# Half of NSA's output projection moved into the last attention turn, an unscaled first convolution product, merged exponentials and another order of pieces

## The reference, cut to what matters

```python
def conv_mixer(a, state, w_in, w_conv, w_out):        # a = rmsnorm(x, g)
    gb, gc, v = jnp.split(a @ w_in, 3, axis=-1)
    u = gc * v
    ...
def nsa_merge(gates, o_c, o_s, o_w, w_out):
    o = gates[:, :, 0, ..., None] * o_c + gates[:, :, 1, ..., None] * o_s + gates[:, :, 2, ..., None] * o_w
    b, t = o.shape[:2]
    return o.reshape(b, t, N_HEADS * HEAD_DIM) @ w_out
```

## Time and profile before

| | us |
|---|---|
| median of 3 runs | 1237.3 (1236.7 to 1241.01) |
| the profiled execution, its own time | 1240.33 |
| its span, first to last instruction | 1238.6 |
| PE busy | 1179.3 (95%) |
| DVE busy | 476.5 (38%) |
| ACT busy | 282.7 (23%) |
| POOL busy | 220.8 (18%) |

### The profile page before, as it was taken

The page is one execution under the profiler, slowest core; times in us unless marked ns, Lnnn a source line. Parts: engine busy times, 40 slices in busy tenths (PEclk is TensorE's granted clock), DMA queues, the critical chain, the costliest instruction groups (busy, mean ns, idle before and its releaser), DMA issues.

```text
span 1238.6 us, 36557 instructions
## 1 busy us (share of the span) xinstructions
PE 1179.3 (95%) x14710; PEld 967.6 (78%) x14710; DVE 476.5 (38%) x1370; ACT 282.7 (23%) x755; POOL 220.8 (18%) x376
## 2 busy tenths in 40 slices
PE   8999999999999999999788779999999999999998
PEld 6877876999999977874345447797887987978966
DVE  2110115676775323005778773441121211211223
ACT  1000003110110022325877861310011011010131
POOL 4033242011340000413355540100000000000000
PEclk9999999999999999999999999999999999999999
DMA  9998889999442474653687789599999999999721
GB/s 328 307 311 282 300 284 320 170 364 334 141 163 97 179 288 154 175 104 102 205 278 241 240 259 356 216 375 366 378 343 368 362 366 393 334 353 389 295 102 39
DMA packets 122955, 329.99 MB, mean 266 GB/s; under 512 B 17864, under 2 KB 56729, under 8 KB 121124
## 3 DMA queue, kind: packets, MB, share of 16 engines
q1 hardware_dynamic: 96628, 259.88, 57.6%
q0 software_dynamic: 16656, 59.30, 16.5%
q10 hardware_dynamic: 9504, 8.48, 2.4%
HBM read 319.16 MB, written 15.70 MB: 270 GB/s over the span
## 4 chain that ended last, share of the span: by engine, by line
PE 80%; issue 6%; SPq 4%; DMA 4%; POOLq 2%; POOL 2%; DVE 1%; ACT 1%; DVEq 0%; ACTq 0%
PE bank L2715 16%; PE bank L2048 16%; PE bank L2155 12%; PE pbank L2726 6%; PE bank L2191 6%; PE pbank L2715 3%; PE bank L2726 3%; PE bank L2106 3%; PE bank L2259 3%; SPq L630 2%; POOLq L630 2%; DMA gring<-in_dense_gu 1%; PE bank L2667 1%; DMA gring<-in_conv_in 1%; SPq L640 1%
## 5 line engine op out<-in xcount | busy, mean ns | idle before, releaser
L2715 PE MATMUL bank<-X,gring 128*64 128x96 f32 x4608 | 197.5, 246 | 6.2 <-issue 5.8
L2715 PEld LDWEIGHTS bank<-X,gring 128*64 128x64 f32 x4608 | 192.6, 137 | 11.6 <-issue 11.4
L2048 PE MATMUL bank<-aT,gring 128*128 128x288 f32 x736 | 183.3, 407 | 4.9 <-DMA gring<-in_conv_in 3.1
L2048 PEld LDWEIGHTS bank<-aT,gring 128*128 128x128 f32 x736 | 138.9, 190 | 44.3 <-DMA gring<-in_conv_in 3.6
L2726 PE MATMUL pbank<-Q,X 128*32 128x256 f32 x1152 | 78.1, 379 | 0.0
L640 POOL DMA_DIRECT2D Q<-in_cache_cmp x96 | 51.8, 539 | 123.0 <-issue 123.0
L2155 PE MATMUL bank<-aT,gring 128*128 128x144 f32 x528 | 72.3, 286 | 0.0
L1974 DVE TENSOR_TENSOR X<-X,bank 128x96 f32<-128x96 f32 x72 | 18.4, 256 | 134.1 <-ACT X L1328 132.2
L1967 DVE TENSOR_TENSOR hT<-hT,bank 128x288 f32<-128x288 f32 x48 | 18.9, 449 | 129.0 <-PE bank L2667 129.0
L2155 PEld LDWEIGHTS bank<-aT,gring 128*128 128x128 f32 x528 | 67.8, 190 | 0.3 <-issue 0.3
L2048 PE MATMUL bank<-Q,gring 128*128 128x288 f32 x256 | 63.3, 408 | 1.3 <-ACT tS L957 0.7
(11 more groups left out here) (394 smaller groups left out, 1794.6 us busy)
## 6 DMA issues: line engine op xcount, KB each, us to landing
gring<-in_moe SPq DMA_DIRECT2D x176, 512.0 KB, 6.0
Q<-in_moe SPq DMA_DIRECT2D x72, 512.0 KB, 7.4
gring<-in_dense_gu SPq DMA_DIRECT2D x44, 512.0 KB, 12.4
gring<-in_conv_in SPq DMA_DIRECT2D x24, 512.0 KB, 7.2
Q<-in_cache_cmp POOLq DMA_DIRECT2D x96, 128.0 KB, 4.2
Q<-in_cache_cmp SPq DMA_DIRECT2D x96, 128.0 KB, 4.0
gring<-in_dense_down SPq DMA_DIRECT2D x16, 704.0 KB, 5.4
Q<-in_cache_cmp ACTq DMA_DIRECT2D x64, 128.0 KB, 3.8
```

What stands on the lines that cost most here:

```text
L2048: ins = pe.matmul(bank(label, k)[:, 0:T], tile[:, 128 * i:128 * i + 128], rhs[:, i, :], start=i == 0, stop=i == C - 1)
L2715: ins = pe.matmul(m_bank(i, M_GU + f)[64 * w:64 * w + 64, CAP * u:CAP * u + CAP], gslot(("m", 0), 2 * f + u)[:, o:o + 64], ae[:, c, :], st ...
```

## The change

Four edits.

1. **First product.** DVE makes xg0 = x times gain, without the factor 1/rms, while the squares are still summed; PE multiplies ("gc", 0) with xg0 right behind the norm, and DVE applies the factor when it takes the result out of the bank (ACT copied it before). The zeros are three, then one behind the second and one behind the fourth step of the norm. SP waits for ("gc", 0) before it loads w_cmp, which shares memory with xg0.
2. **Half of the output projection.** Head groups 0 to 3 are complete before turn 3. In turn 3, half_out(c) multiplies their 4 chunks of weights with the 256 prompt tokens for each of the 8 output chunks, and half_added(c) adds the bank to h. The final pass has 4 chunks by 288 tokens and 4 by the 32 sample tokens. The weights for it are loaded twice: four tiles ("wa", i) are put in the ring behind sv(2, 2) and behind sv(2, 3), each of two DMAs of 256 KB on SP.
3. **Merged exponentials.** The compressed branch of the prompt has one exponential of 32 columns instead of four of 8 with an accumulated sum; DVE subtracts the maxima first and sums afterwards.
4. **Order.** In each turn ACT does prompt_exps(2p, 0) ahead of key_scale(p, 2), and all five exponentials of the selected branch one after the other; PE does T6, window_keys, importance, T2, prompt_transposes, T5, prompt_transposes, T3, T4; DVE does window_scores behind prompt_transposed(2p, 0).

```diff
--- before.py
+++ after.py
@@ g_tile_order
             if p:
                 o += [("sv", p - 1, u, b2) for u in VALUES_AT[t] for b2 in range(2)]
+            if p == 3 and t >= 2:
+                o += [("wa", 2 * (t - 2) + i) for i in range(2)]
@@ g_released
+            elif kind == "wa":
+                full(eng, ("wa", 2 * label[1] + 1))
@@ sync
+            full(sp, ("gc", 0))
             for k in range(2):
                 sp.dma_start(wc[:, 32 * k:32 * k + 32, :], A["w_cmp"][:, 32 * k:32 * k + 32, :]).then_inc(wcmp_in, 16)
...
+                elif label[0] == "wa":
+                    n = GN[label]
+                    g_released(sp, g_labels[n - GS])
+                    for i in range(2):
+                        sp.dma_start(gslot(label)[:, 512 * i:512 * i + 512], A["nsa_out"][2 * label[1] + i][:, 0:512]).then_inc(g_in[n % GS], 16)
@@ scalar, prompt_exps
                 if i == 0:
-                    for w in range(2):
-                        for q in range(2):
-                            act.activation(Scp[:, w, q, :], Scp[:, w, q, :], ACT.Exp, bias=nmp[:, w, q, 0:1],
-                                           accum_out=smp[:, w, q, 0:1]).then_inc(pexp_ready, 1)
+                    act.activation(Scp, Scp, ACT.Exp).then_inc(pexp_ready, 1)
@@ scalar, turn p
                 key_scale(p, 1)
+                key_squares(p, 4)
+                key_squares(p, 5)
                 if p:
                     prompt_exps(2 * p - 1, 1)
                 if p == 0:
                     token_values(1)
-                key_squares(p, 4)
-                key_squares(p, 5)
-                key_squares(p, 6)
+                prompt_exps(2 * p, 0)
                 key_scale(p, 2)
...
                 exps(1, SN[p % 2], smt[:, 4:5], sexp_ready)
+                if p < 3:
+                    key_squares(p + 1, 1)
                 exps(1, S[:, 0:512], smt[:, 0:1], sexp_ready)
+                exps(1, S[:, 512:1024], smt[:, 1:2], sexp_ready)
+                exps(1, S[:, 1536:2048], smt[:, 3:4], sexp_ready)
+                exps(1, S[:, 1024:1536], smt[:, 2:3], sexp_ready)
@@ vector
             dve.wait_ge(first_in, 16 * NFIRST)
+            for c in range(C):
+                dve.wait_ge(x_in[c // 2], 16)
+                dve.tensor_scalar(xg0[:, c, :], hT[:, c, :], gains[:, c:c + 1], None, ALU.mult).then_inc(xg_sums_ready, 1)
             norm(0)
...
+            full(dve, ("gc", 0))
+            drain(dve.tensor_tensor(sg[:, 0, :], bank(("gc", 0))[:, 0:T], rs[:, 0, :], ALU.mult), ("gc", 0))
...
-                dve.wait_ge(pexp_ready, 12 * (k + 1))
+                dve.wait_ge(pexp_ready, 9 * (k + 1))
+                chain(dve.tensor_reduce(smp[:, :, :, 0], Scp, AX.X, ALU.add))
+                settled()
...
+            def half_added(c):
+                full(dve, ("wa", c))
+                drain(dve.tensor_tensor(hT[:, c, 0:TP], hT[:, c, 0:TP], bank(("wa", c))[:, 0:TP], ALU.add), ("wa", c))
@@ tensor
-            norm(0)
+            for c in range(C):
+                norm_step(0, c)
+                if c in (1, 3):
+                    warm(1)
+            g_arrived(pe, ("gc", 0))
+            for c in range(C):
+                pe.wait_ge(xg_sums_ready, c + 1)
+                ins = pe.matmul(bank(("gc", 0))[:, 0:T], gslot(("gc", 0))[:, 128 * c:128 * c + 128], xg0[:, c, :],
+                                start=c == 0, stop=c == C - 1)
+            fill(ins, ("gc", 0))
...
+            def half_out(c):
+
+                g_arrived(pe, ("wa", c // 2))
+                bank_free(pe, ("wa", c))
+                for k in range(4):
+                    drained(pe, ("po", k))
+                    o = 512 * (c % 2) + 128 * k
+                    ins = pe.matmul(bank(("wa", c))[:, 0:TP], gslot(("wa", c // 2))[:, o:o + 128], oT[:, k, 0:TP],
+                                    start=k == 0, stop=k == 3)
+                fill(ins, ("wa", c))
...
             for c in range(C):
-                g_linear(("wo", c), oT)
+                g_arrived(pe, ("wo", c))
+                bank_free(pe, ("wo", c))
+                for k in (4, 5, 6, 7, 0, 1, 2, 3):
+                    first = 0 if k >= 4 else TP
+                    ins = pe.matmul(bank(("wo", c))[:, first:T], gslot(("wo", c))[:, 128 * k:128 * k + 128], oT[:, k, first:T],
+                                    start=k == 4, stop=k == 3)
+                fill(ins, ("wo", c))
```

More of the change, by code:

```diff
@@ L562, in trunk @@
             other = by_pool(label) or label[0] in ("skip", "d")
-            landed.append((landed[n - GS] if n >= GS else 0) + (0 if other else 64 if four else 16))
+            landed.append((landed[n - GS] if n >= GS else 0) + (0 if other else 64 if four else 32 if label[0] == "wa" else 16))
             pool_landed.append((pool_landed[n - GS] if n >= GS else 0) + (64 if by_pool(label) else 0))
@@ L1005, in _ @@
             for c in range(C):
[L1006 removed]
                 if c >= 2:
                     drained(act, ("v", c - 2))
[L1009 removed]
+                if c:
+                    full(act, ("gc", c))
+                    drain(act.activation(sg[:, c % 2, :], bank(("gc", c))[:, 0:T], ACT.Copy), ("gc", c))
                 if c == 0:
+                    full(act, ("gc", 0))
                     pages(early_pages, 1)
@@ L1248, in _ @@
                     token_values(2)
+                key_squares(p, 6)
+                if p == 0:
                     folded_values()
                 transposed(p, 0)
-                prompt_exps(2 * p, 0)
                 key_squares(p, 7)
@@ L1278, in _ @@
                 transposed(p, 3)
-                if p < 3:
-                    importance(p + 1)
                 transposed(p, 4)
-                transposed(p, 2)
                 if p < 3:
@@ L2110, in _, with warm @@
             pe.wait_ge(constants_set, 1)
-            for _ in range(6):
-                pe.matmul(bank(("norm", 0))[:, 0:T], zeros[:, 0:128], zeros[:, 128:128 + T], start=True, stop=True)
+            def warm(n):
+                for _ in range(n):
+                    pe.matmul(bank(("v", 0))[:, 0:T], zeros[:, 0:128], zeros[:, 128:128 + T], start=True, stop=True)
+            warm(3)
             pe.wait_ge(first_in, 16 * NFIRST)
-            norm(0)
+            for c in range(C):
[8 more added lines that the diff above has]
+            fill(ins, ("gc", 0))
             for c in range(C):
                 for name in ("gc", "v", "gb"):
-                    g_linear((name, c), aT, ready=0 if c == 0 and name == "gc" else None)
+                    if (name, c) != ("gc", 0):
+                        g_linear((name, c), aT, ready=0 if (name, c) == ("v", 0) else None)
                 if c >= 2:
@@ L2583, in _ @@
                     selected_values(p - 1, 3)
+                if p == 3:
+                    half_out(0)
                 prompt_logits(2 * p + 1, 1)
+                if p == 3:
+                    half_out(1)
+                transposes(p, 6)
+                if p == 3:
+                    half_out(2)
                 if p < 3:
                     window_keys(p + 1)
-                transposes(p, 6)
-                transposes(p, 3)
-                if p < 3:
                     importance(p + 1)
                 transposes(p, 2)
+                if p == 3:
+                    half_out(3)
                 prompt_transposes(2 * p, 0)
+                if p == 3:
+                    half_out(4)
                 transposes(p, 5)
-                transposes(p, 4)
                 if p:
@@ L2597, in _ @@
                 prompt_transposes(2 * p, 1)
+                if p == 3:
+                    half_out(5)
+                transposes(p, 3)
+                if p == 3:
+                    half_out(6)
+                transposes(p, 4)
+                if p == 3:
+                    half_out(7)
                 prompt_values(2 * p)
```

98 lines of the change are left out of this document (58 added, 40 removed).

## The result

| | median of 6, us | all, us |
|---|---|---|
| before | 1239.95 | 1236.7 to 1241.69 |
| after | 1248.75 | 1245.66 to 1255.97 |

The ratio is estimated from all runs: 1.0095, 95% interval 1.0071 to 1.0119, which is 9 to 15 us slower. The quotient of the two medians, 1.0071 (8.8 us), is its lower end. The forecast was 1241.8, in a range of 1231.5 to 1247.5, and "no change" as the likeliest. The profiled execution of the changed kernel took 1255.97, the longest of the six, with a span of 1254.3.

The account below looks back on a forecast made before the run. PE, working in 95% of the span, was taken to bound the kernel. Start -2.1, order +0.8, pieces +10.1, load wait +4.1, clock +1.7 and final pass -10.1 gave +4.5 on 1237.3: 1241.8 us, range 1231.5 to 1247.5.

Parts of the forecast that it names:

- The start: Convolution's first product: with the norm begun behind three zeros, it ends at 14.6 and not 16.7 us, -2.1.
- all waits in the block of the pieces are filled: Turn 3, behind pv(2, 3): 3.8 us of PE's waits go because PE now comes later.
- The block's growth: Turn 3: eight pieces of the projection take 13.9 us, less 3.8 of filled waits, +10.1.
- the wait for pp(1, 0): Behind turn 3: SP's last twelve pages wait for half_out(3), so PE waits 4.7 us instead of 0.64, +4.1.
- The clock's fall behind that wait: Ahead of attention's tail: the wait of 4.7 us makes the granted clock fall to 0.50 again, +1.7.
- the one on the order: Attention's turns, merged exponentials and new order: +0.8 for all, from -1.5 to +2; key_scale(0, 2) 1 to 2 us later.
- The final pass: Output projection: 64 instructions of 288 columns and 64 of 32 at 0.087 us take 21.2 us, not 31.28, -10.1.
- What is won or lost up to 785 us is kept: Experts behind the projection: they hang on PE too, so earlier gains and losses carry through to the end.
- D: Slower rival: new tiles push turn 3's pages back, up to 5.3 us more, 1247.1 us; chance 0.18.
- B: Rival: the wait for pp(1, 0) stays near 0.6 us and the clock stays, -1.3, 1236.0 us; chance 0.22.
- C: Faster rival: pieces fill turn 3's whole idle 7.5 us, no wait for pp(1, 0), -7.8, 1229.5 us; chance 0.15.

Follow-up runs that it names:

- e7: Kernel before with only the half of the output projection added (its tiles, pieces and two-part pass): 1253.94 us, ratio 1.0136.
- e2: Changed kernel with prompt_exps(0, 0) of turn 0 back in its old place, behind transposed(0, 0): 1250.04 us, ratio 1.0097.
- e6: Changed kernel with turn 0's exponentials in their old place and pp(1, 0) loaded ahead of the last sixteen pages: 1240.4 us, ratio 1.0024.
- e12: Changed kernel without the half of the projection and with turn 0's exponentials in their old place: 1236.19 us, ratio 0.9995.
- e13: e12 with SP's first loads for the experts held until the third product of the projection is done: 1232.19 us, ratio 0.9955.
- e14: e6 with 17 products without use (8.3 us) added behind the projection: 1246.84 us, ratio 1.0073.
- e8: Kernel before with one edit, prompt_exps(0, 0) ahead of key_scale(0, 2) in turn 0: 1240.95 us, ratio 1.0046.
- e11: Kernel before with the half of the projection, and pp(1, 0) loaded ahead of the last pages: 1245.52 us, ratio 1.0065.
- e4: Changed kernel without the half of the projection and its four extra tiles; first product, merged exponentials and order stay: 1240.62 us, ratio 1.0024.
- e3: Changed kernel with pp(1, 0) ahead of the sixteen pages of sv(3, t) in the ring and SP's list: 1246.34 us, ratio 1.0065.

## Why the prediction was wrong, by its own steps

**Right.** The start: "-2.1", measured -2.0 in the first profile (-1.7 to -3.2 over the eleven with this edit). That all waits in the block of the pieces are filled: measured, none left in the changed kernel (1.5 us are in e7, with the old order). The block's growth "+10.1": +11.3, of which the fall of the clock at its start is about the difference. The mechanism of the wait for pp(1, 0), with half_out(3) as its gate and twelve pages of SP behind it: 19.1 us forecast from there to the landing, and 739.1 to 759.2, 20.1 measured. The clock's fall behind that wait.

**The step that failed first** is the one on the order, "I take +0.8 for all". It said that key_scale(0, 2) would come "1 to 2 us" later. In the changed kernel it came 3.5 us later relative to the start of attention, because DVE's scores were 5 us behind ACT and not "a little". In the trace of before, DVE waits 4.55 us for POOL's mask of turn 0 and then works 3.5 us before it comes to the scores at 587.92, when ACT's key_scale(0, 2) (587.82) had already begun:

```profile
584.37 3.51 DVE L1805 CUSTOM_DVE_ANT_0 X<-X,small 128x512 f32<-128x512 f32 x1 [4.55 <-POOL X L899]
587.92 0.18 DVE L1667 TENSOR_TENSOR sg<-pbank,tabC 128x16 f32<-128x16 f32 x1
```

A to M3 is 141.1 in the mean of five profiles with this place of the exponentials and 136.4 in five without it (e2, e6, e12, e13, e14): 4.6 us for one misplaced group (3.0 in the old order, e8's 141.0 against 138.0), against which the rest of the new order and the merge seem to win 1.6 (136.4 against 138.0 in five profiles of the old order; these two groups meet at 137.0 to 137.3). The term was +3.1 (+2.3 in the two first profiles), and its range ended at +2. The rows above would have told; I had bounded the time of DVE's maxima by eye.

**The terms that were mis-sized**, all to the same side. The wait: 4.1 forecast, 5.5 and 4.8 measured (the landing took 6.47 in place of 5.78). The clock behind it: 1.7 against 2.8 and 2.1, since the wait itself passed at the low level and the whole product behind it too. The final pass: -10.1 against -8.5. There the 64 instructions of 32 columns cost (22.82 - 15.6) / 64 = 0.113 us each and not 0.087. The 0.087 came from a misreading of the earlier trace rows: a count in a window holds every instruction that touches it. Here x12 in 1 us are 9 that start in it and 3 that had begun before; over 3 us of the same instructions the view counts

```profile
515.70:518.70 3.00, 3.00 (x29) 1.00 0.44 163
```

and their starts stand 0.112 us apart. At that pace the short ones take 7.2 us, the pass 22.8 and the term is -8.5, as measured. The short instructions stand eight in a row behind eight long ones, and in the trace of the changed kernel they start 0.111 us apart: 32 columns cost what 48 do. The wait for the values ahead of the block, not counted at all, grew by 1.5 and 2.8; the stretch from M3 to those values grew by 0.15 and 1.4, since PE came to them earlier.

Put together for the two first spans, the 11.2 us by which +15.7 exceeds the forecast's +4.5 are: start 0.4, order 1.5, values 0.15, block 1.2, wait 1.4, clock 1.1, final pass 1.6, and 3.8 behind the projection.

**The step that can't be held.** "What is won or lost up to 785 us is kept" was the basis for all sums, and its 3.8 us are the largest single miss. Behind the projection the routing took some 1.6 us more in ten of the sixteen profiles, with and without the half, with the clock at 0.50 there, and the stretch to the end lies between 449.2 and 459.2 us over all of them (456.9 and 451.9 for the changed kernel itself). With the half it is some 5 us longer in the mean. That is seen, and not explained; the loads of the first expert are ruled out by e13. It stays open.

**The rivals.** D named the new tiles pushing the pages back, to be told by over 1.7 us more wait ahead of pv(2, 3). That wait ends when POOL's last page of those values lands, which POOL issues 20.5 to 20.6 us behind its mask in all sixteen profiles. In the old order it then lands in 4.9 to 5.4 us in four profiles without the tiles and in 6.5 and 7.9 in the two with them (e7, e11), where the wait is 2.9 and 4.2 us and not 0.9 to 1.4: D happened there. In the new order it takes 5.0 to 6.8 without them (e4, e12, e13) and 4.7 to 7.1 with them, and the wait is 1.1 to 3.8 and 0.5 to 4.1, so there these profiles can't tell the tiles from scatter. B's and C's condition, that pp(1, 0) is not waited for, did not hold; where e3 and e11 make it hold, the half costs 5.7 (e3 against e4) and 8.8 us, and not the 10.1 - 10.1 = 0 that B's sum has for it. The range was too narrow above: nearly all terms were off to the costly side, what comes behind the projection had no term, and the yardstick was an execution with one fall of the clock.

## What to carry to other kernels

Moving work into idle time pays only up to the idle time, and it pushes what stands behind it in every queue: here 3.8 us of 13.9 were covered, the second pass cost more for each column, and one tile at the end of SP's list made a wait of 6 us that an earlier place in the ring takes away. When a group moves up in one engine's list, look up when its input is ready before pricing it; one merged exponential (four in e8) in the wrong place of turn 0 moved the mask of turn 3 by 3 to 4.6 us. When a rate is read from a count in a window, take a long window or the starts. Take two profiles of the kernel before where a change of 0.5% is at stake.

## What the runs showed of the hardware

The granted clock also falls when no wait of PE shows. Near 516 us PE was busy 2.00 of 2.00 us, in products of 48 columns, and the clock was 0.50; nor is there a gap in the 16 us ahead of it:

```profile
500.00:510.00 10.00, 10.00 (x43) 1.00 0.76 209
510.00:520.00 10.00, 10.00 (x65) 0.83 0.59 194
```

It fell there in both profiles of the changed kernel, in e2, e3 and e7, and in none of the other eleven, whose products there are the same. The page of the Trainium skill named above, in that section and in "A second HAM failure mode: psum-queue depth-cycling", puts the falls in its kernels down to idle time, in long waits or in many small gaps; for this one the trace shows neither. The cause is open.

Falls are also not equal to lost time: e12 has a mean clock of 0.9912 over its runs and 1236.19 us, e6 0.9949 and 1240.4.

Float32 instructions with 128x128 weights that stand in a row start 0.11 us apart whether they have 32 columns (0.111, the final pass) or 48 (0.112); with 288 columns it is 0.244.

And delaying ten loads of 512 KB by 13 us (e13) gave the fastest of all versions, 0.9955 (0.9930 to 0.9979) of before.
